# Inner FFN projections as one-level Strassen products of a 2x2 block pair

## The reference

```python
def rmsnorm(x, g):
    xf = x.astype(jnp.float32)
    r = lax.rsqrt(jnp.mean(xf * xf, axis=-1, keepdims=True) + EPS)
    return (xf * r).astype(x.dtype) * g

def conv_ffn(h, conv_prev, w_in, conv_w, conv_b, w_out):
    T = h.shape[1]
    u, gate = jnp.split(h @ w_in, 2, axis=-1)
    ext = jnp.concatenate([conv_prev.astype(u.dtype), u], axis=1)
    a = conv_b + sum(ext[:, j:j + T] * conv_w[j] for j in range(CONV_W))
    out = (jax.nn.silu(a) * gate) @ w_out
    return out, ext[:, -(CONV_W - 1):]
```

## Time and profile before

| | us |
|---|---|
| runs, median (lowest to highest) | 1646.18 (1644.73 to 1647.42) |
| profiled execution, span | 1641.1 |
| TensorE matmul busy | 1594.7 |
| VectorE busy | 869.0 |
| ScalarE busy | 631.5 |
| GpSimd busy | 294.3 |

### The profile page before, as it was taken

How to read it: one execution, slowest core, us unless ns; L and a number is a source line. 1 busy time by engine, 2 the same in 40 slices (tenths; PEclk the granted TensorE clock), 3 DMA queues, 4 the chain that set the end, 5 groups by cost and what they waited for, 6 DMA issues and landing times. The chain is left out here.

```text
span 1641.1 us, 36066 instructions
## 1 busy us (share of the span) xinstructions
PE 1594.7 (97%) x14126; PEld 1517.9 (92%) x14126; DVE 869.0 (53%) x1522; ACT 631.5 (38%) x1003; POOL 294.3 (18%) x355
## 2 busy tenths in 40 slices
...
GB/s 203 74 85 80 80 80 93 69 79 82 78 82 84 81 85 77 85 84 83 93 117 119 121 103 141 220 314 327 123 79 88 77 89 77 89 77 93 99 99 29
DMA packets 52291, 173.97 MB, mean 106 GB/s; under 512 B 7202, under 2 KB 8754, under 8 KB 52194
## 3 DMA queue, kind: packets, MB, share of 16 engines
...
## 5 line engine op out<-in xcount | busy, mean ns | idle before, releaser
L1554 PE MATMUL acc<-xl,w_hi 128*128 128x288 f32 x2160 | 474.3, 301 | 10.2 <-DVE w_lo L1000 10.2
L1554 PE MATMUL acc<-xh,w_hi 128*128 128x288 f32 x2160 | 463.1, 296 | 0.0
L1554 PE MATMUL acc<-xh,w_lo 128*128 128x288 f32 x2160 | 463.0, 296 | 0.0
L816 DVE TENSOR_TENSOR w_lo<-w_raw,w_hi 128x1024 fp32r<-128x1024 f32 (+1 forms) x215 | 277.0, 1288 | 333.2 <-ACT w_hi L447 332.1
L1554 PEld LDWEIGHTS acc<-xl,w_hi 128*128 128x128 f32 x2160 | 348.4, 189 | 17.7 <-DVE w_lo L1000 10.2
L1554 PEld LDWEIGHTS acc<-xh,w_hi 128*128 128x128 f32 x2160 | 348.7, 189 | 0.0
L1554 PEld LDWEIGHTS acc<-xh,w_lo 128*128 128x128 f32 x2160 | 348.4, 189 | 0.0
L447 ACT ACTIVATE w_hi<-w_raw 128x1024 fp32r<-128x1024 f32 (+1 forms) x215 | 222.6, 1035 | 301.8 <-PE acc L1554 269.7
L1554 PE MATMUL acc<-ffn_glo,w_hi 128*128 128x288 f32 x704 | 151.1, 295 | 0.0
L1554 PE MATMUL acc<-ffn_gh,w_lo 128*128 128x288 f32 x704 | 149.8, 293 | 0.0
L1554 PE MATMUL acc<-ffn_gh,w_hi 128*128 128x288 f32 x704 | 148.9, 293 | 0.0
...
## 6 DMA issues: line engine op xcount, KB each, us to landing
w_raw<-w_fi_in SPq DMA_DIRECT2D x88, 512.0 KB, 3.5
w_raw<-w_fo_in SPq DMA_DIRECT2D x32, 512.0 KB, 3.5
dec_Kd<-cache_k_in SPq DMA_DIRECT2D x32, 512.0 KB, 5.3
att_Vd<-cache_v_in SPq DMA_DIRECT2D x32, 512.0 KB, 5.3
w_raw<-w_mix_in SPq DMA_DIRECT2D x31, 512.0 KB, 3.5
w_raw<-w_o_in SPq DMA_DIRECT2D x16, 512.0 KB, 3.5
w_raw<-w_kv_in SPq DMA_DIRECT2D x16, 512.0 KB, 3.5
w_raw<-w_qg_in SPq DMA_DIRECT2D x16, 512.0 KB, 3.5
```

The source lines that it names most:

```text
L816: nc.vector.tensor_tensor(w_lo[:, pos.slot % SPL, 0:width], w_raw[:, pos.slot, 0:width], w_hi[:, pos.slot % SPL, 0:width].bitcast(F32), AL ...
L1554: mm = nc.tensor.matmul(dst[:, hf, 0:HALF], W[:, sp_, 128 * (j0 + j):128 * (j0 + j) + 128], X[:, kt, HALF * hf:HALF * hf + HALF], start=(f ...
```

## The change

Four pairs of a layer stay as they were but for what is added to them. For the other 18, x is normalised first (`x_scaled`: h times gain times rms, in fp32), and the 2x2 of (u, gate weights) x (first and second half of the inner dimension) times the 2x2 of (halves of the inner dimension) x (halves of the 576 tokens) is made with 7 products for 8, in the form with 4 sums of x, 4 sums of weights and 7 additions of results. Each product is 4 x 3 matmuls of 128x128 by 288.

- The x side is made once per layer, in the plain pairs: 4 tiles, each with two scalings (VectorE), four 288-wide sums (GpSimd), three hi copies (ScalarE), three lo subtractions (VectorE).
- Per fast pair GpSimd makes four 512-wide weight sums, ScalarE and VectorE split them and the parts of the raw blocks that products use.
- Results lie in four PSUM banks. ScalarE copies partial results out (`snap`), VectorE adds to them: three additions for u, two for the gate (`gt`). No product with rms is left; GpSimd multiplies silu by the gate.
- The products stay in fp32 (`g0`, `gx`) and are split in the last pair and behind it, by 22 copies and 22 subtractions, into space that x sums had. The first output tile waits for them one by one.
- The two samples' filter taps are joined with the prompt's: one 592-wide instruction for two. u has two buffers.
- Raw blocks of the fast pairs are loaded when the sums two pairs earlier are split. Semaphores of the key stage are merged (fb_ok, flf_ok, c16_ok, cl_ok and others into logit_ok, two k_out into one) with the same order of work.

```diff
+PLAIN = 4
+FAST = FT - PLAIN
...
+        gx = Region("ffx", x_at)("gx", [P, FT - 6, T])
+        gt = sq
+        snap5, snap2, snap4 = ssq[:, 0:HALF], ssq[:, HALF:T], rms[:, 0:HALF]
...
+                plain(b_in, 2 * PLAIN + 4, d[f"w_fi{layer}"])
+                with sp.Fori(3, FT // 2) as i:
+                    for k in range(2):
+                        for j in (2 * k, 2 * k + 1):
+                            load(Pos(b_in + j, i, 4), row_of(d[f"w_fi{layer}"], 4 * i + j),
+                                 ready=(s_lo, of_w(layer, FAST * layer, 3) + 8 * i + 4 * k - 20))
+                sp.wait_ge(s_ok, of_w(layer, FAST * (layer + 1), 4))
...
+                def x_hi_parts(j):
+                    r = DT // 2 * layer + j
+                    act.wait_ge(xn_ok, r + 1)
+                    nc.scalar.activation(xsh[:, 0, j], xn[:, 0, 0:HALF], ACT.Copy).then_inc(s_hi, 1)
+                    nc.scalar.activation(xsh[:, 1:3, j], xn[:, 1].rearrange("p (a n) -> p a n", a=2), ACT.Copy).then_inc(s_hi, 1)
+                    act.wait_ge(s_ok, of_x(r, 4) + 4)
+                    nc.scalar.activation(xsh[:, 3:7, j], traw[:], ACT.Copy).then_inc(s_hi, 1)
...
+                def fast_pair(k, i, last=False):
+                    f = 2 * i + k
+                    n, s, nk, ni = FT * layer + f, FAST * layer + f - PLAIN, 1 - k, i + k
+                    b1 = b_in + 2 * f
+                    act.wait_ge(grp_ps, 5 * s + 1)
+                    act.wait_ge(c2_ok, 2 * n - 2)
+                    act.wait_ge(cst_ok, 2 * n - 2)
+                    nc.scalar.activation(u[:, k, 2:2 + HALF], aux[:, k, 0:HALF], ACT.Copy).then_inc(snap_ok, 1)
+                    act.wait_ge(grp_ps, 5 * s + 2)
+                    act.wait_ge(evac, t_in + 2 * f)
+                    nc.scalar.activation(snap5, aux[:, 3, 0:HALF], ACT.Copy).then_inc(snap_ok, 1)
+                    if last:
+                        act.wait_ge(s_lo, of_w(layer, FAST * (layer + 1), 3))
+                        g_hi(0)
...
+                        sum_hi(0, s + 1)
+                        act.wait_ge(grp_ps, 5 * s + 3)
+                        u_hi(nk, ni)
+                    act.wait_ge(grp_ps, 5 * s + 4)
+                    nc.scalar.activation(snap2, aux[:, k, 0:HALF], ACT.Copy).then_inc(snap_ok, 1)
+                    if last:
+                        hi(Pos(b_out), ready=(grp_ps, 5 * s + 3))
+                        g_hi(2)
+                    else:
+                        sum_hi(1, s + 1)
...
+                    act.wait_ge(grp_ps, 5 * s + 5)
+                    nc.scalar.activation(snap4, acc[:, 1, 1, 0:HALF], ACT.Copy).then_inc(snap_ok, 1)
+                    if last:
+                        for m in range(3, 7):
+                            g_hi(m)
+                    else:
+                        gate_hi(nk, ni)
+                        act.wait_ge(block_done, b1 + 1)
+                        sum_hi(2, s + 1)
+                    conv_first(k, f)
...
+                        act.wait_ge(block_done, b1 + 2)
+                        sum_hi(3, s + 1)
+                        silu(f)
...
+                def x_scaled(j):
+                    r = DT // 2 * layer + j
+                    wait(dve, s_ok, of_x(r, 4))
+                    wait(dve, s_hi, of_x(r, 3))
+                    wait(dve, s_lo, of_x(r, 3))
+                    for half in range(2):
+                        m = j + half * DT // 2
+                        op = nc.vector.scalar_tensor_tensor(out=xn[:, half], in0=h[:, m], scalar=gains[:, G_FFN + 8 * layer + m:G_FFN + 8 * layer + m + 1],
+                                                            in1=rms[:], op0=ALU.mult, op1=ALU.mult)
+                    op.then_inc(xn_ok, 1)
...
+                    if f == 0:
+                        x_scaled(0)
                     lo(Pos(b_in + 2 * k + 2, i, 4))
...
+                    taps(k, f)
+                    if f == 1:
+                        x_lo_parts(1)
+                        x_scaled(2)
+                    if f == 2:
+                        x_scaled(3)
+                    if f < PLAIN - 1:
+                        lo(Pos(b_in + 2 * k + 3, i, 4))
+                    dve.wait_ge(silr_ok, PLAIN * layer + f + 1)
...
+                    nc.vector.tensor_tensor(halves(g0[:, f]), acc[:, 1 - tp, :, 0:HALF], halves(sil[:]), ALU.mult).then_inc(prod_ok, 1)
                     dve.wait_ge(prod_ok, n + 1)
                     nc.vector.sem_inc(evac, 1)
...
+                    if f == 0:
+                        x_lo_parts(0)
+                        x_scaled(1)
+                    if f == 1:
+                        x_lo_parts(2)
+                    if f == 2:
+                        x_lo_parts(3)
+                    if f == PLAIN - 1:
+                        s0 = FAST * layer
+                        sum_lo(0, s0)
+                        sum_lo(1, s0)
+                        gate_lo(0, 2)
+                        sum_lo(2, s0)
+                        sum_lo(3, s0)
...
+                def fast_pair(k, i, last=False):
+                    f = 2 * i + k
+                    n, s, nk, ni = FT * layer + f, FAST * layer + f - PLAIN, 1 - k, i + k
+                    b1 = b_in + 2 * f
+                    if not last:
+                        sum_lo(0, s + 1)
+                    dve.wait_ge(grp_ps, 5 * s + 3)
+                    dve.wait_ge(snap_ok, 4 * s + 1)
+                    nc.vector.tensor_tensor(u[:, k, 2:2 + HALF], u[:, k, 2:2 + HALF], aux[:, 2, 0:HALF], ALU.add)
+                    if last:
+                        for m in range(3):
+                            g_lo(m)
+                        lo(Pos(b_out))
+                    else:
+                        lo(Pos(b_in + 2 * nk, ni, 4))
+                        sum_lo(1, s + 1)
+                        gate_lo(nk, ni)
+                    dve.wait_ge(block_done, b1 + 1)
+                    dve.wait_ge(snap_ok, 4 * s + 3)
+                    nc.vector.tensor_tensor(u[:, k, 2 + HALF:2 + SEQ], aux[:, 3, 0:SEQ - HALF], snap2[:, 0:SEQ - HALF], ALU.add)
+                    nc.vector.tensor_tensor(samples(k), aux[:, 3, SEQ - HALF:HALF].rearrange("p (n t) -> p n t", n=NSEQ),
+                                            snap2[:, SEQ - HALF:HALF].rearrange("p (n t) -> p n t", n=NSEQ), ALU.add).then_inc(u_ok, 1)
+                    dve.wait_ge(u_ok, n + 1)
+                    nc.vector.sem_inc(evac, 1)
+                    if last:
+                        g_lo(3)
+                    else:
+                        sum_lo(2, s + 1)
+                    taps(k, f)
+                    dve.wait_ge(block_done, b1 + 2)
+                    dve.wait_ge(snap_ok, 4 * s + 4)
+                    dve.wait_ge(prod_ok, n)
+                    nc.vector.tensor_tensor(gt[:, 0:HALF], aux[:, k, 0:HALF], snap4, ALU.add)
+                    nc.vector.tensor_tensor(gt[:, HALF:T], aux[:, k, 0:HALF], snap5, ALU.add).then_inc(evac, 1)
+                    if last:
+                        for m in range(4, 11):
+                            g_lo(m)
+                        lo(Pos(b_out + 1))
+                        for m in range(11, FT):
+                            g_lo(m)
+                    else:
+                        sum_lo(3, s + 1)
...
+                def x_sums(j):
+                    r = DT // 2 * layer + j
+                    pool.wait_ge(xn_ok, r + 1)
+                    wait(pool, s_lo, of_x(r, 3))
+                    b11, b12, b21, b22 = xn[:, 0, 0:HALF], xn[:, 0, HALF:T], xn[:, 1, 0:HALF], xn[:, 1, HALF:T]
+                    nc.gpsimd.tensor_tensor(traw[:, 1], b12, b11, ALU.subtract).then_inc(s_ok, 1)
+                    nc.gpsimd.tensor_tensor(traw[:, 3], b22, b12, ALU.subtract).then_inc(s_ok, 1)
+                    pool.wait_ge(s_ok, of_x(r, 4) + 1)
+                    nc.gpsimd.tensor_tensor(traw[:, 2], b22, traw[:, 1], ALU.subtract).then_inc(s_ok, 1)
+                    pool.wait_ge(s_ok, of_x(r, 4) + 3)
+                    nc.gpsimd.tensor_tensor(traw[:, 0], b21, traw[:, 2], ALU.subtract).then_inc(s_ok, 1)
...
+                def weight_sums(k, i, first):
+                    pu, pg_ = Pos(b_in + 2 * k, i, 4), Pos(b_in + 2 * k + 1, i, 4)
+                    s = FAST * layer + 2 * i + k - PLAIN
+                    wu, wg = w_raw[:, pu.slot], w_raw[:, pg_.slot]
+                    if first:
+                        pool.wait_ge(s_lo, of_w(layer, s, 3) - 3)
+                        pool.wait_ge(w_in[pg_.slot], 16 * pg_.lap + 16)
+                        nc.gpsimd.tensor_tensor(Sw[:, 0], wg[:, 0:512], wg[:, 512:1024], ALU.add).then_inc(s_ok, 1)
+                        pool.wait_ge(s_lo, of_w(layer, s, 3) - 2)
+                        pool.wait_ge(w_in[pu.slot], 16 * pu.lap + 16)
+                        pool.wait_ge(s_ok, of_w(layer, s, 4) + 1)
+                        nc.gpsimd.tensor_tensor(Sw[:, 1], Sw[:, 0], wu[:, 0:512], ALU.subtract).then_inc(s_ok, 1)
+                    else:
```

(100 more changed lines are left out.)

287 lines of the change are left out of this document (184 added, 103 removed).

## The result

The changed kernel takes 1698.16 us (median; 1696.72 to 1699.39), the kernel before 1645.45 us beside it (1643.31 to 1647.42). The ratio is 1.032, 95% interval [1.030, 1.033]: 3.2% slower, where 1693 us had been forecast (2.8% over the 1646.2 us that the kernel before had then). The profiled execution has a span of 1696.8 us for 1641.1.

The account below looks back on a forecast made before the run. TensorE bounded the kernel before; VectorE, blocked by GpSimd on shared SBUF ports, would bound fast pairs. Per layer +20.8 entry, -2.0 pairs, -1.6 last pair, +6.3 end: +23.5; two layers +47, span 1688.1, median 1693 us, range 1638 to 1740.

Parts of the forecast that it names:

- What bounds: Whole kernel: TensorE's instruction rate bounds it before; after the change VectorE's blocked line sets the fast pairs, 12.6 us each.
- The fast pair: 18 changed pairs per layer: 12.60 us a repeating pair against 12.73 before, with TensorE idle 1.5 us before its fourth product.
- The walk: Instructions laid end to end along VectorE's line: 7.2 us own time, 3.6 blocked, 1.8 waiting, 12.6 us a fast pair.
- The entry: Four plain pairs and first fast pairs: the x chain delays u evacuations and stalls TensorE, +20.8 us a layer.
- A hole of over 5 us: Sign expected in the entry: one TensorE gap over 5 us among 3 us holes; the walk had 5.7 us.
- The last pair and the end: Stage end: last pair 11.1 us, -1.6; late product splits stall TensorE 1.2, 1.0, 2.2, 1.9 us, +6.3 a layer.
- The likeliest case: Fast pairs: VectorE's line with blocks, 12.1 to 13.0 us a pair, 1675 to 1715 us (also given as 1669 to 1715); chance 0.6.
- Rival 1: Fast pairs: ports leave room, TensorE sets 11.1 us a pair; 1648 us with the forecast entry, down to 1615; chance 0.25.
- Rival 2: Fast pairs: every port hand-over costs in full, 13.6 us a pair, +43 us a layer, 1733 us; 0.15 shared with rival 3.
- Rival 3: Entry: stalls lower TensorE's clock, 0 to 5 us a layer, up to 1703 us, counted as 0; 0.15 shared with rival 2.
- Rival 4: Fast pairs: product groups of 12 run slower than 132 ns a matmul; up to 1.5 us a pair hidden; no chance given.
- The forecast's own tests: Signs: GpSimd sums 1.6 to 2.2 us, half VectorE's subtractions 1.4 to 1.8, u evacuations 12.6 apart, idle put to ScalarE's snapshot.

Follow-up runs that it names:

- e1: Changed kernel with VectorE's two-SBUF-input instructions in fast pairs reading one operand from an idle PSUM bank; 1640.7 us, kernel before beside it 1651.9.
- e2: Changed kernel with GpSimd's four weight sums per fast pair replaced by a 16-column subtraction and a memset each; 1636.8 us, kernel before 1651.9.

## Why the prediction was right

**What bounds.** Right: 36 pairs with 12 matmuls fewer gave nothing, because VectorE's line and not TensorE sets the fast pair. e1 and e2 show that in the pairs it is only the shared reads. One reading was beside the point: for a matmul the prediction took 122.5 ns from the Trainium skill ("TensorE: Matmul & The Clock Gate", Back-to-back issue gap). The Trainium skill gives that formula there for an isolated matmul and says that in a stream with a weight load for each matmul both set the spacing, as they may here; nothing in the sum used it.

**The fast pair.** 12.60 us forecast, 12.93 measured; the mechanism is right and the size off by 0.33 x 15 = 5 us a layer. In the pair from 556.73 to 569.75 (13.02 us) the blocked time is 0.52 + 0.72 + 1.08 + 1.86 = 4.2 us: the four instructions above against 0.69, 1.23, 0.69 and, for both taps with the 0.15 between them, 1.81. The walk had 3.6; four of its five blocks are right within 0.1 (0.95 + 0.83, 0.70, 1.06), and the term that was mis-sized is the fifth, 0.08 us forecast for the first sum's split and 0.52 measured, since GpSimd's product (557.89 to 559.43) was still running when that split was issued at 558.77. VectorE's own time is 7.5 for 7.2, because the 0.09 us of overlap were taken off all 13 instructions, also those that wait and so overlap with nothing. The waits are 1.3 for 1.8; a hop from ScalarE's copy to VectorE's split is 0.03 us in the rows (558.74 to 558.77), for the walk's 0.08. TensorE's idle ahead of the fourth product is 1.52 for 1.5, on the engine and the line that were named.

**The entry.** Steps of 17.3, 20.0 and 15.9 us forecast, 17.26, 19.59 and 15.65 measured. TensorE's gaps in layer 0, as the distance between two matmuls less the usual 0.13 (0.16 to 0.32 us more than the timeline's idle marks), are 4.3, 1.9, 2.9, 2.8, 4.2, 2.4 and 1.6 us, 20.1 for the 22.8 of the forecast: close in sum, less so one by one. A hole of over 5 us is there only in layer 1 (5.35). The entry's whole cost isn't measured by itself; as what is left of 25.9 with the other terms as measured (+3.0 pace, -2.4 last pair, +5.5 end) it is 19.8, for 20.8.

**The last pair and the end.** 10.33 us in place of 11.1 for the last step (-2.4 for -1.6), stalls, as distances again, of 0.73, 0.90, 2.13 and 1.78 for 1.2, 1.0, 2.2 and 1.9. In sum 1.6 us better a layer.

**The sum.** 23.5 us a layer forecast, 25.9 and 25.4 measured: the pace's +5.0 less 2.6 of the other terms. So the span, forecast at 1688.1 and measured at 1696.8, has 4.3 us more from the two stages and 4.4 from outside them, for which nothing had been counted. The median is 1.4 us above the span, not 5.1, which takes 3.7 of it back; that the forecast of the median is 5 us off and that of the span 8.7 is luck. The two belong together: an execution's own time is 1.6 us over its span (1698.43 for 1696.8), so the profiled execution of the kernel before took some 1642.7 us, less than any of its four runs beside the changed kernel (1643.3 to 1647.4). The medians differ by 52.7 us, of which the stages are 51.3, so most of the 4.4 us is probably the scatter of one execution, and adding 5.1 to a span was an error of the sum. The likeliest case's lower end stands in the prediction twice, as 1675 and as 1669; by its own terms 12.1 us a pair would give 1678. Nothing hangs on it.

**The rivals.** Rival 1 (TensorE's pace) is what e1 and e2 built, and its time was 1648 us with the entry kept; they came out at 1641 and 1637. On paper 10.8 of 11.1 us of the ports' time fitted; the trace says that this sum of two engines' shares is no schedule. Rival 2 (13.6 a pair) didn't occur: from 562.14 to the end of GpSimd's sum at 563.36 are 1.22 us, but the split begun at 562.14 is only 1.77 - 0.69 = 1.08 longer, so 0.14 us of it ran while it was blocked. The Trainium skill ("SBUF — State Buffer", SBUF: two separate sides) has the first of the two hold the pair of ports for the whole instruction and the other fully blocked; this trace agrees but for that 0.14 us. Rival 3 (the clock) did occur. In the entry the granted clock is at the lower of its two levels (1.2 GHz) for 10.2 us in layer 0, from 421, 455 and 462 us, and for 13.7 us in layer 1, from 1271, 1291 and 1312 us; in the stages of the kernel before it never is. Ahead of the first, from 416 to 421 us, TensorE was busy for 0.91 us. Windows (length, TensorE busy and its instructions; behind the engines the granted clock, DMA share, GB/s; the last three are TensorE's alone):

```profile
416.00:421.00 5.00, 0.91 (x7) 0.67 (x6) 3.11 (x6) 1.83 (x2) 4.76 (x6) 1.00 0.00 0
...
420.00:424.00 4.00, 3.54 (x17) 3.54 (x18) 2.79 (x4) 1.94 (x5) 2.29 (x3) 0.66 0.51 131
```
```profile
455.00:459.00 4.00, 3.18 (x12) 0.57 0.00 0
...
1291.00:1296.00 5.00, 5.00 (x29) 0.66 0.38 108
1312.00:1319.00 7.00, 5.88 (x24) 0.51 0.01 2
```

Two matmuls inside such a stretch, 0.24 us apart:

```profile
456.20 0.44 PE L2080 MATMUL aux<-ffn_xsl,w_hi 128*128 128x288 f32 x1
456.44 0.44 PE L2080 MATMUL aux<-ffn_xsh,w_lo 128*128 128x288 f32 x1
```

At most half of it, 5 us in layer 0 and 7 in layer 1, could be lost, and the entry came out no dearer than forecast, so most of it fell into time in which TensorE would have waited. Layer 1 has 3.4 us more of the low clock and its stage is 0.6 us shorter, which fits that. No run here separates it. Rival 4 didn't occur: at the full clock matmuls are 0.13 us apart inside the groups.

**The forecast's own tests.** GpSimd's sums at 1.66 to 2.24 us, the 512-wide subtractions at 1.5 in half their cases, idle put down to the snapshot: all there. u evacuations 12.6 apart: 12.9.
